# The output projection of a SwiGLU feed-forward part, done by seven block products over pairs of inner rows

## The reference

```python
h = rms_norm(x, g_pre_mix)
hc, bg, cg, q, k, v = split(h @ w_in, 6)                      # 1024 x 3072
y = concat(group_rms_norm(short_gated_conv(hc, bg, cg)), group_rms_norm(chunked_band_attention(q, k, v)))
x = x + rms_norm(y @ w_out, g_post_mix)
h = rms_norm(x, g_pre_ffn)
gate, up = split(h @ w_ffn_in, 2)                             # w_ffn_in: 1024 x 5632
f = (silu(gate) * up) @ w_ffn_out                             # w_ffn_out: 2816 x 1024
x = x + rms_norm(f, g_post_ffn)
```

## Time and profile before

| | |
|---|---|
| median of three runs | 1204.44 us (1204.34 to 1204.47) |
| the profiled execution, device time | 1204.4 us |
| its span, first to last instruction | 1202.6 us |
| mean granted TensorE clock | 0.997 |
| matmuls | 5963 |

### The profile page before, as it was taken

How to read it: one execution, slowest core, us unless ns; L and a number is a source line. 1 busy time by engine, 2 the same in 40 slices (tenths; PEclk the granted TensorE clock), 3 DMA queues, 4 the chain that set the end, 5 groups by cost and what they waited for, 6 DMA issues and landing times.

```text
span 1202.6 us, 16371 instructions
## 1 busy us (share of the span) xinstructions
PE 1172.6 (98%) x5963; PEld 980.0 (81%) x5963; DVE 625.4 (52%) x1132; ACT 447.3 (37%) x844; POOL 96.8 (8%) x126
## 2 busy tenths in 40 slices
PE   7999999999999999999999999999999999999996
PEld 6978878888878887778888888888888888888885
DVE  5333334244333547795566565666656533338336
ACT  5433433433344536763233322323332323243321
POOL 3201000100100013310000000000000110001000
PEclk9999999999999999999999999999999999999999
DMA  8211010111100153450322223222121492345421
GB/s 274 78 36 36 18 54 18 36 36 36 36 25 30 35 193 132 165 174 8 118 78 79 87 70 105 67 90 87 53 70 35 146 362 87 105 158 184 150 86 71
DMA packets 91874, 111.35 MB, mean 93 GB/s; under 512 B 3488, under 2 KB 73128, under 8 KB 91824
## 3 DMA queue, kind: packets, MB, share of 16 engines
q1 hardware_dynamic: 83488, 80.23, 20.9%
q0 software_dynamic: 7184, 26.26, 5.8%
q10 hardware_dynamic: 1152, 4.19, 0.9%
HBM read 93.87 MB, written 16.80 MB: 92 GB/s over the span
## 4 chain that ended last, share of the span: by engine, by line
PE 94%; DVE 2%; ACT 2%; issue 1%; DMA 1%; POOL 1%; SPq 0%; ACTq 0%; DVEq 0%; POOLq 0%
PE psum L929 32%; PE psum L629 25%; PE psum L834 25%; PE psum L658 4%; PE psum L652 3%; PE psum L644 2%; PE psum L620 1%; DMA raw<-in_w_in 1%; ACT misc L1012 1%; DVE ws L1413 1%; PE psum L767 1%; PE psum L761 0%; DVE arena L1664 0%; ACT arena L1213 0%; POOL x2rs L498 0%
## 5 line engine op out<-in xcount | busy, mean ns | idle before, releaser
L629 PE MATMUL psum<-hT,ws 128*128 128x512 f32 (+1 forms) x1512 | 333.8, 373 | 2.2 <-DVE arena L1673 1.1
L629 PEld LDWEIGHTS psum<-hT,ws 128*128 128x128 f32 x1512 | 255.1, 189 | 44.8 <-issue 2.7
L834 PE MATMUL psum<-ws,hT 128*128 128x512 f32 x1056 | 239.8, 389 | 0.4 <-DVE hT L1812 0.4
L834 PEld LDWEIGHTS psum<-ws,hT 128*128 128x128 f32 x1056 | 198.1, 188 | 42.0 <-DVE ws L1413 0.8
L929 PE MATMUL psum<-arena_r,ws 128*128 128x512 f32 x960 | 224.1, 389 | 0.0
L929 PEld LDWEIGHTS psum<-arena_r,ws 128*128 128x128 f32 x960 | 180.2, 188 | 37.4
L1413 DVE TENSOR_TENSOR ws<-raw,ws 128x1024 fp32r<-128x1024 f32 x90 | 110.0, 1223 | 148.6 <-ACT ws L1336 125.9
L929 PE MATMUL psum<-hT,ws 128*128 128x512 f32 x720 | 169.8, 389 | 0.0
L929 PEld LDWEIGHTS psum<-hT,ws 128*128 128x128 f32 x720 | 135.1, 188 | 28.1
L1765 DVE TENSOR_TENSOR misc<-misc,psum 128x512 f32<-128x512 f32 x100 | 68.6, 686 | 105.6 <-PE psum L929 105.5
L1336 ACT ACTIVATE ws<-raw 128x1024 fp32r<-128x1024 f32 x44 | 46.7, 1060 | 150.1 <-PE psum L834 132.3
(11 more groups left out here) (151 smaller groups left out, 1020.6 us busy)
## 6 DMA issues: line engine op xcount, KB each, us to landing
raw<-in_w_ffn_in SPq DMA_DIRECT2D x44, 512.0 KB, 3.8
raw<-in_w_ffn_out SPq DMA_DIRECT2D x44, 512.0 KB, 3.2
raw<-in_w_in SPq DMA_DIRECT2D x24, 512.0 KB, 3.8
raw<-in_w_out SPq DMA_DIRECT2D x18, 512.0 KB, 3.2
arena<-in_x SPq DMA_DIRECT2D x16, 512.0 KB, 8.7
act_scratch<-arena POOLq DMA_DIRECT2D x16, 512.0 KB, 2.9
arena<-act_scratch POOLq DMA_DIRECT2D x16, 512.0 KB, 6.5
x_scratch<-arena ACTq DMA_DIRECT2D x8, 512.0 KB, 2.6
```

The costliest lines, as they stand in the source:

```text
L629: last = mm(PP[pair][:, at:end], w[wp], hT[:, hp, k, at:end], start=(k == 0 and (wp, hp) == (0, 0)), stop=(k == KT - 1 and wp == 1))
L834: last = mm(pair[:, half * 512:(half + 1) * 512], ap[:, tile * P:(tile + 1) * P], ws[:, slot, wp, half * 512:(half + 1) * 512], start=(fir ...
```

## The change

The output projection becomes a 2x2 block product as well. A pair of inner rows (2i, 2i+1) and the even and odd token tiles are the blocks of the activation (`act11` row 2i of even tiles, `act21` row 2i of odd tiles, `act12`, `act22` the same of row 2i+1); the two inner rows and the two column halves of 512 are the blocks of the weight (`wb11` to `wb22`). There are 11 pairs (`NP`) and seven products per pair; so 77 chunks of 12 matmuls each take the place of 44 chunks of 24.

1. During the feed-forward input, VectorE makes four sums of activation blocks (`sum_acts`, in the first unit of each pair, for the pair before) and four sums of weight blocks (`sum_weights`, in the second unit, for the pair to come), one instruction of 128x512 each. They stand between the instructions of `ffn_in`. After the two plain rows VectorE makes the weight sums of pair 0.
2. GpSimd's queue loads two rows of `w_ffn_out` per pair, and stores four weight sums (`weight_scratch`), three activation blocks and four activation sums (`act_scratch`), 256 KB each. It waits for the landing of the weight sums' stores before it loads the next rows. All activations go through DRAM now.
3. Activation rows are kept in one pair of SBUF rows only. So `times_silu` waits for stores of the pair before: the first one of a unit for `acts_stored`, and the second one in the first unit of a pair for `s_stored`, the landing of all four activation sums that were made in the same unit.
4. The projection runs pass by pass over the seven products (each over 11 pairs), from a ring of six buffers. SyncE loads each chunk as two transfers of 256 KB. ScalarE makes two high parts of 128x512 per chunk, VectorE two low parts.
5. Passes write to PSUM banks 4 to 7 and 0 to 3 in turn; between them ScalarE copies, or VectorE adds, the finished product's four banks (`copy_out`, `sum2`, `sum3`, `q21`, `q22`, `q11`), in the first four chunks of the next pass. The odd token tiles are finished in passes 5 and 6, the even ones at the end.
6. The last four chunks are again done tile by tile, now 12 matmuls a tile. The inverse root moves from VectorE to GpSimd (three operations for an even tile), and it is applied after the gain.
7. `x2` (the residual) and the post-norm gain are loaded by GpSimd's queue, 9 transfers of 512 KB, after the last pair's sums have been stored; before, the same data came in two groups of four, with the gain ahead of them. SyncE's loads of pass 1 (chunk 11) wait for these stores too.
8. The loops over the projection's chunks are written out in full on every engine; before, most of the chunks ran in hardware loops.

```diff
-            for c in range(4):
-                ffn_out(0, c, 0, c == 0, False)
-            with pe.Fori(1, 5) as r:
...
+            def out_tile(c, n):
+                p, i = c // NP, c % NP
+                (ah, al), (bh, bl) = w_op(c % 4 * 2), w_op(c % 4 * 2 + 1)
+                for a, b in ((ah, bh), (ah, bl), (al, bh)):
+                    last = mm(out_bank(p, n), a[:, n * P:(n + 1) * P], b, ...)
...
+            for c in range(CHUNKS - 4):
+                pe.wait_ge(out_split, 2 * c + 2)
+                for n in range(4):
+                    if c % NP == 0:
+                        bank_free(c // NP, n)
+                    last = out_tile(c, n)
+                last.then_inc(out_done, 1)
```

VectorE in a unit (`more(k)` is one `sum_acts` or one `sum_weights`):

```diff
                 low_op(n + 1, 1), low_op(n + 1, 2)
+                more(0), more(1)
                 add_bank(n, 5, c22, u3, BANK[3], c22_made)
+                more(2)
                 low_op(n + 1, 3), low_op(n + 1, 4)
                 add_bank(n, 6, u3, u3, BANK[2], c21_made)
+                more(3)
                 low_op(n + 1, 5)
-                times_silu(n, out, 0, s11, u3, sil1_done, free)
+                times_silu(n, j, 0, s11, u3, sil1_done, acts_stored, i * 48 + 48)
                 add_bank(n, 7, u2, u2, BANK[3], c12_made)
                 low_op(n + 1, 6)
-                times_silu(n, out, 1, u2, c22, sil2_done)
+                times_silu(n, j, 1, u2, c22, sil2_done, s_stored if j == 0 else acts_stored,
+                           i * 64 + 64 if j == 0 else i * 48 + 48)
```

GpSimd's queue:

```diff
-            for j in range(SPILLED):
-                pool.wait_ge(act_done, 2 * j + 2)
-                pool.dma_start(act_d[j * P:(j + 1) * P, :], row(16 + j % 2)).then_inc(act_stored[j % 2], 16)
...
+            for i in range(NP):
+                pool.wait_ge(ta_made, 4 * i + 4)
+                for p, src in ((1, t2), (2, t3), (3, t4), (4, t1)):
+                    pool.dma_start(t_block(p, i), src).then_inc(t_stored, 16)
+                pool.wait_ge(t_stored, 64 * (i + 1))
+                if i < NP - 1:
+                    load_w(i + 1)
+                pool.wait_ge(act_done, 4 * i + 4)
+                for p, src in ((0, act11), (5, act12), (3, act22)):
+                    pool.dma_start(a_block(p, i), src).then_inc(acts_stored, 16)
+                pool.wait_ge(sa_made, 4 * i + 4)
+                for p, src in ((1, as2), (2, as3), (4, as1), (6, as4)):
+                    pool.dma_start(a_block(p, i), src).then_inc(s_stored, 16)
```

SyncE's loads, and ScalarE's and VectorE's split:

```diff
+            for c in range(CHUNKS):
+                p, i = c // NP, c % NP
+                to = raw_ring[c % RING]
+                if c < 3:
+                    sp.wait_ge(w_split, W0 - 1)
+                elif c < RING:
+                    sp.wait_ge(prod, OPS * ROUNDS)
+                else:
+                    sp.wait_ge(out_split, 2 * (c - RING) + 2)
...
+            for c in range(4, CHUNKS):
+                high_chunk(c, out_done, c - 3)
...
+            for c in range(4, CHUNKS):
+                low_chunk(c)
```

More of the change, by code:

```diff
@@ new lines, in mean_factor @@
+            def mean_factor(n):
+                chain(nc.gpsimd.tensor_scalar(var_pool[:, :], var_pool[:, :], 1.0 / D, EPS, ALU.mult, ALU.add))
+                factors_to(rst[:, n:n + 1], var_pool[:, :], 1, f_rs, n + 1)
+            for n in range(4):
+                pool.wait_ge(f_sq, n + 1)
+                chain(nc.gpsimd.tensor_copy(var_pool[:, :], ssq[:, 24 + n:25 + n]))
+                mean_factor(n)
+            for n in range(4):
+                pool.wait_ge(out_ready, n + 1)
+                pool.dma_start(out_d[(2 * n + 1) * P:(2 * n + 2) * P, :], row(ODD_ROWS + n)).then_inc(out_stored[n], 16)
@@ L606, in _ @@
+            for n in range(4):
+                pool.wait_ge(f_sq, 9 + n)
+                chain(nc.gpsimd.tensor_tensor(var_pool[:, :], ssq[:, 28 + n:29 + n], ssq[:, 16 + n:17 + n], ALU.add))
+                mean_factor(4 + n)
             for n in range(4):
@@ L823, in out_pair, with down @@
                 return i % 4 if i < 6 else i - 4
-            def down(slot, a, tiles, pairs, width, phase, first, last_k, done, signal=True):
-                hi, lo = a_slot(a, width, phase)
+            def down(slot, a, tiles, pairs, width, first, last_k, done, signal=True):
+                hi, lo = a_slot(a, width)
                 for n, tile in enumerate(tiles):
@@ L1338, in ffn_high, with high_chunk @@
[L1338 to L1342, removed]
-                if with_w:
-                    high_w(landed, c + 2, chunk_used, r + USED0 + c - 1)
+            def high_chunk(c, done, value):
+                act.wait_ge(chunk_landed[c % RING], 32 * (c // RING + 1))
+                act.wait_ge(done, value)
+                for part in range(2):
+                    if c == 3 and part == 1:
+                        act.wait_ge(t_stored, 64 * NP)
+                    go(w_op(c % 4 * 2 + part)[0], raw_ring[c % RING][:, part * 512:(part + 1) * 512], ACT.Copy
+                       ).then_inc(out_hi, 1)
@@ L1870, in _, with first_half, second_half, sum2 @@
-            for c in range(40, 44):
-                ffn_low(0, c, 1, c - NF - KEPT, c < 42)
-            for i in range(4, NT):
-                norm_f(i)
+            times_silu(n, 1, 1, u2, c22, sil2_done, acts_stored, 48 * (NP - 1))
+            low_chunk(3)
+            def first_half(rows, n):
+                return row(rows + n, 512)
+            def second_half(rows, n):
+                return row(rows + n, 512, 512)
+            def sum2(n):
+                dve.wait_ge(out_done, 2 * NP)
+                dve.wait_ge(first_copied, n + 1)
+                tt(second_half(EVEN_ROWS, n), first_half(EVEN_ROWS, n), out_bank(1, n), ALU.add).then_inc(sum2_made, 1)
```

433 lines of the change are left out of this document (231 added, 202 removed).

## The result

| | before | changed | ratio, 95% interval |
|---|---|---|---|
| median (4 executions each) | 1204.45 us | 1191.57 us (1190.1 to 1192.4) | 0.9892 (0.9875 to 0.9909) |
| profiled execution / its span | 1204.4 / 1202.6 | 1190.1 / 1188.3 | |

The kernel became faster by 1.1% where 2.6% was forecast; 1191.6 lies above the range.

What follows compares the result with a forecast made beforehand. The prediction took TensorE, busy 98% of the span, to bound the kernel. It summed 1204.4 - 29.9 (matmuls) + 0.3 (last pair) - 0.2 (last four chunks) - 1.0 (tail) = 1173.6 us, with a range of 1171.5 to 1181.

Steps and rivals of the forecast that it cites:

- Matmuls removed: Projection on TensorE: 132 fewer matmuls at 0.2268 us each, -29.9 us; three in a row on one bank cost nothing.
- VectorE's sums in a unit: Feed-forward units: the added sums bring VectorE to 24 instructions, 78% of a unit, and cost the path 0.
- The wait for the activation sums' stores: Second `times_silu` of a pair's first unit: VectorE waits some 2 us for four stores, TensorE not at all, 0.
- T' + 6.1: Latest start of the second `times_silu` that costs TensorE nothing, in us after the next unit's product 0 starts (T').
- the middle case, 5.1: Landing of the four activation sums' stores, at T' + 5.1, between a lower end of T' + 3.0 and an upper of T' + 7.4.
- Rival A: Units: the activation sums' stores, served one by one, land late; 13 us in 10 pairs, 1186.6 us; chance 9%.
- Projection's supply: Projection: SyncE's chunk loads, needing 193 GB/s, and the splitting into high and low parts keep up with TensorE; 0.
- rival B: Small waits where TensorE's queue changes over (passes, start, written-out code): 4 to 7 us, 1179 us; chance 9%.
- Rival C: Projection: the ring runs dry as 256 KB transfers don't overlap, 4.0 us per chunk, 1272 us, slower than before; chance 4%.
- Last pair: End of the units: three chunk loads beside the activation sums' stores make these land at about 5.5 to 6.5; +0.3 us.
- Last four chunks: End of the projection: TensorE waits 0.2 us ahead of these chunks instead of 0.45; -0.2 us.
- Tail: From the last matmul's end to VectorE's last end: 5.2 us instead of 6.15, -1.0 us (bounds -1.3 to +1.7).

Runs made afterwards that it cites:

- both_fixes: Changed kernel with the in-place sum's store issued first and waited for alone, and residual and gain loads after pass 1: 1174.80 us, ratio 0.9751.
- late_x2: Changed kernel with the loads of residual and gain started only after pass 1 of the projection: 1187.43 us, ratio 0.9859.
- own_buffer: Changed kernel with an own SBUF place for the sum made in place of `act21`, second `times_silu` not waiting for the sums' stores: 1179.09 us, ratio 0.9786.
- small_both: Changed kernel with both inner weight loads of each unit cut to an eighth (stale weights): 1177.89 us, one execution.
- small_load: Changed kernel with the second inner weight load of each unit cut to an eighth (stale weights): 1178.37 us, one execution.
- small_first: Changed kernel with the first inner weight load of each unit cut to an eighth (stale weights): 1189.63 us, one execution.
- as3_first: Changed kernel with the in-place sum stored ahead of two others under its own semaphore, `times_silu` waiting for that store only: 1177.19 us, ratio 0.9771.
- own_late: Changed kernel with an own buffer for the in-place sum, and residual and gain loads after pass 1: 1175.52 us, ratio 0.9758.

## Why the prediction was wrong, point by point

**Matmuls removed, -29.9: right.** In both_fixes and late_x2 924 matmuls take 210.08 us; 209.5 was forecast, and there is a short wait ahead of the last four chunks in it. So three matmuls in a row on one bank, and code written out in full, cost half a microsecond at most.

**VectorE's sums in a unit, 0: right.** own_buffer shows 380.80 us. VectorE's load rose to 290.56 of 394.40 us in the changed kernel and 289.69 of 380.80 in both_fixes, 76%; 78% was forecast, from a miscount: a unit had 18 of these instructions and not 20, by the code and by the 355 and 63% of the earlier trace rows, and has 22 now.

**The wait for the activation sums' stores, 0: the step that failed.** The prediction's chain behind the wait was right link by link, and so was its limit of T' + 6.1. What failed is the landing, "I take the middle case, 5.1". Measured were T' + 6.3 in the first pair and up to T' + 7.6 later (836.37 in the seventh, T' being 828.75), for two reasons.

- The way from issue to landing takes 7.1 to 7.5 us (8.4 in the first pair of late_x2); 5.7 was forecast (from T' - 0.6 to 5.1). In these 5.7 the four stores by themselves had 4.0: 2.7 for their bytes, 0.9 to the first data and 0.4 for the notice, and no row shows the last two. They take 4.8 (small_both). The second weight load adds 2.5 us (small_load against small_first), where I had its 1.7 us. Both terms were too low by 0.8.
- The delay feeds on itself, up to a point. The fourth sum ended at T' - 1.1 in the first two pairs, near the forecast 0.9, but at T' - 0.1 in the sixth. A late `times_silu` makes the whole following unit of VectorE late, its low parts too, and SyncE loads the next raw weights only when these are done; so `s_first` waits for them in the next pair (7.1 us in seven pairs), the sums come late, their stores later still. TensorE's gap before product 3 grew with it and then fell: none shown, 0.57, 1.03, 1.36, 1.25, 1.39, 1.49, 1.07, 0.62, 0.98. The ninth pair has no wait for raw weights ahead of its sums, and its stores go out 0.8 us before T' again. In as3_first the stores' bytes are the same, but the first delay is missing, and so is the wait for raw weights (0.3). The prediction reckoned one pair and multiplied by ten. That the raw weights close the loop is read from these two traces; no run broke the loop at that point alone.

**Rival A, 1186.6, was the case**, with its price almost to the point: 13 us against 13.55. But its mechanism, stores served one by one in 8.0 us, was not: alone they take 4.8. And the price was not 1.3 us in each pair but 0.3 in the first and 1.8 in the seventh (from 798.66 to 838.56 it is 39.90 us, and two units are 38.08). So that the sums agree is partly luck. Nine in a hundred was too little where the middle estimate kept clear of the limit by only 1.0 us and rested on a single transfer of another queue.

**Projection's supply, 0: wrong by 2.4 to 4.1 us**, a piece of rival B. Two steps failed. "If SyncE gets half of 384 GB/s": it got 38%, and a third while both queues were full. And the 4.7 MB and chunk 11 were to come "at about 14 us": both came at 19.5, since the stores before them again landed later than reckoned. SyncE's own rate and all pass changes were right. Rival C did not come: SyncE's queue brings what is needed when it has the transfer engines to itself.

**Last pair, +0.3:** 0.6 to 0.8 in the two kernels where it can be seen apart.

**Last four chunks, -0.2: right.** TensorE waits 0.1 us there in both_fixes, where it was 0.45 and 0.2 was forecast.

**Tail, -1.0: right up to VectorE's last end, wrong behind it.** From the last matmul's end (1180.0) to VectorE's last end, 1185.19, it is 5.2 us, as forecast:

```profile
1181.78 0.66 POOL L668 TENSOR_TENSOR var_pool<-ssq 128x1 f32<-128x1 f32 x1 [0.81 <-ACT misc L1071]
...
1182.53 0.58 POOL L656 TENSOR_SCALAR var_pool<-var_pool 128x1 f32<-128x1 f32 x1
...
1183.19 0.55 POOL L544 TENSOR_TENSOR rst<-var_pool,mhalf 128x1 f32<-128x1 f32 x1
...
1184.44 0.75 DVE L1960 SCALAR_TENSOR_TENSOR arena<-arena,rst 128x512 f32<-128x512 f32 x1
```

GpSimd's three operations took their short form, 0.55 to 0.66 each. But the span behind the last matmul fell by 0.3 only, not by 1.0 (8.3 against 8.6): from VectorE's end to the span's end it is 3.1 us where it was 2.4. The trace shows what ends last. Each queue closes with a DRAIN; before, then after:

```profile
L105 POOLq DRAIN  x1: 12466/12466/12466, 1108.7 to 1108.7; - x1
...
L105 SPq DRAIN  x1: 13/13/13, 1202.4 to 1202.4; - x1
```

```profile
L107 POOLq DRAIN  x1: 4150/4150/4150, 1183.9 to 1183.9; - x1
L107 SPq DRAIN  x1: 7/7/7, 1187.5 to 1187.5; - x1
```

Before, GpSimd was through long ahead of the end, and SyncE closed the span. Now GpSimd makes the last inverse root, so its DRAIN begins at 1183.9, lasts 4.15 us and ends at 1188.1, 0.6 behind SyncE's. This is read from the traces; no run leaves the last root on VectorE. "The final store is unchanged" missed that another queue could end last.

With both losses cured the forecast sum nearly stands: 1174.8 against 1173.6. Of the 1.2 us, 0.9 are the end behind VectorE's last instruction (1169.5 to 1172.9 in both_fixes, 3.4 us against 2.4).

## What to carry to other kernels

When a buffer is reused while its store is in flight, work out the limit from the consumer back, as here, and then ask of the landing three things: which of the stores the wait really needs, what the other queue issues in the same microsecond, and whether a late landing delays the very loads that make the next one late. A step with 1 us to spare in a loop is not worth 0; it is worth its price times the chance, and the price of a round can grow with the delay of the round before, here from 0.3 to 1.8 us.

A transfer that is needed late should not start when a queue that feeds the critical engine has just been held up: moving the residual's loads behind pass 1 was worth 2.4 to 4.1 us. And an engine that takes over the last small work of a kernel may also end it last: look at every queue's last instruction.

## What the runs showed of the hardware

- The split of the transfer engines between two queues was not half and half by bytes but by packets. From 993 to 1004 us GpSimd's queue moved 822 packets and 3.01 MB, SyncE's 804 packets and 1.47 MB, 2 to 1 in bytes, as their rows are of 4 KB and 2 KB. The Trainium skill, "DMA: Bandwidth & Descriptors", section "Queues, rings and completion order", says that each engine goes round robin between its queues by packet. The trace agrees, with 822 to 804.
- Four stores of 256 KB on GpSimd's queue took 2.13 us to issue and 4.8 us from the first issue to the restart of VectorE, with 64 KB loads beside them (small_both). 512 KB of weight load in 512-byte packets, issued 0.7 us after the first store (789.87 against 789.18), made it 7.3. The load takes 1.7 us of the engines by the earlier trace rows, and cost the stores 2.5.
- A DRAIN at the end of GpSimd's queue took 4.15 us in the changed kernel, 4.40 in as3_first and both_fixes and 5.78 in own_buffer and own_late.
